# Attention weighting in a transformer block: split values as the stationary operand, two heads' probabilities moving, three branches summed in PSUM

## The reference, cut to what matters

```
# p_cmp: softmax over 31 compressed keys; p_sel, p_win: causal softmax over 512 keys
# (with 8 blocks of 64 keys and 16 to choose, every block is chosen, and a window of
#  512 covers all 512 keys: both are full causal attention, with keys and values of their own)
o_cmp = einsum('bghsn,bngd->bsghd', p_cmp, v_compressed)
o_sel = einsum(p_sel, v_sel);  o_win = einsum(p_win, v_win)
gate  = sigmoid(h @ w_gate)                      # 3 per head and token
y_nsa = gate[0]*o_cmp + gate[1]*o_sel + gate[2]*o_win
```

## Time and profile before

| | us |
|---|---|
| median of 3 runs | 2829.82 (2827.25 to 2831.1) |
| span of the profiled execution | 2832.2 |
| PE busy | 2781.4 (98%) |
| DVE busy | 2007.5 (71%) |
| ACT busy | 1158.5 (41%) |
| POOL busy | 62.7 (2%) |

### The profile page before, as it was taken

One profiled execution on the slowest core, in us unless ns is written; L12 is line 12 of the kernel. 1 busy time (PEld: TensorE's weight loads), 2 busy tenths in 40 slices (PEclk: granted clock), 3 DMA queues, 4 the chain that ended last, 5 costly groups with the idle time before them and its releaser, 6 DMA issues.

```text
span 2832.2 us, 41533 instructions
## 1 busy us (share of the span) xinstructions
PE 2781.4 (98%) x16782; PEld 2473.6 (87%) x16782; DVE 2007.5 (71%) x2956; ACT 1158.5 (41%) x1635; POOL 62.7 (2%) x22
## 2 busy tenths in 40 slices
PE   7999999999999999999999999999999999999998
PEld 7888888888888989789898899988999888789897
DVE  4456654544658969589694797875979588669794
ACT  4333444444243424334344443432434357434342
POOL 0000011111000000000000000000000000000000
PEclk9999999999999999999999999999999999999999
DMA  7223312222533333223333233332332343123322
GB/s 221 90 78 105 112 62 84 93 81 97 184 120 98 103 107 111 104 89 105 105 105 106 79 101 109 100 114 69 109 111 93 122 171 110 60 75 107 112 95 75
DMA packets 262192, 295.39 MB, mean 104 GB/s; under 512 B 6210, under 2 KB 248018, under 8 KB 259342
## 3 DMA queue, kind: packets, MB, share of 16 engines
q1 hardware_dynamic: 257008, 281.53, 30.3%
q10 hardware_dynamic: 5022, 11.57, 1.1%
HBM read 276.30 MB, written 16.78 MB: 103 GB/s over the span
## 4 chain that ended last, share of the span: by engine, by line
PE 75%; DVE 20%; issue 3%; ACT 1%; DMA 0%; DVEq 0%; ACTq 0%; SPq 0%
PE bank L1420 13%; PE bank L1422 12%; PE bank L1421 12%; PE bank L1863 5%; PE bank L1865 5%; PE bank L1864 5%; PE bank L1694 5%; PE bank L1752 2%; DVE gate_quarters_lo L2625 2%; DVE up_quarters_lo L2625 2%; PE bank L2026 1%; PE bank L1742 1%; DVE w_lo L2121 1%; PE bank L1435 1%; PE bank L1436 1%
## 5 line engine op out<-in xcount | busy, mean ns | idle before, releaser
L2121 DVE TENSOR_TENSOR w_lo<-w_raw,w_hi 128x2048 fp32r<-128x2048 f32 (+2 forms) x140 | 306.4, 2191 | 138.9 <-ACT w_hi L831 135.7
L1420 PE MATMUL bank<-hid_hi,w_hi 128*128 128x512 f32 x880 | 343.0, 390 | 0.0
L1421 PE MATMUL bank<-hid_lo,w_hi 128*128 128x512 f32 x880 | 342.5, 389 | 0.0
L1422 PE MATMUL bank<-hid_hi,w_lo 128*128 128x512 f32 x880 | 342.4, 389 | 0.0
L831 ACT ACTIVATE w_hi<-w_raw 128x2048 fp32r<-128x2048 f32 (+2 forms) x134 | 243.0, 1820 | 240.0 <-PE bank L1422 161.3
L1420 PE MATMUL bank<-h_hi,w_hi 128*128 128x512 f32 x752 | 298.6, 397 | 3.0 <-DVE w_lo L2121 1.4
L1421 PE MATMUL bank<-h_lo,w_hi 128*128 128x512 f32 x752 | 293.0, 390 | 0.0
L1422 PE MATMUL bank<-h_hi,w_lo 128*128 128x512 f32 x752 | 292.9, 390 | 0.0
L1422 PEld LDWEIGHTS bank<-hid_hi,w_lo 128*128 128x128 f32 x880 | 165.2, 188 | 34.5
L1421 PEld LDWEIGHTS bank<-hid_lo,w_hi 128*128 128x128 f32 x880 | 165.3, 188 | 33.7
L1420 PEld LDWEIGHTS bank<-hid_hi,w_hi 128*128 128x128 f32 x880 | 165.2, 188 | 33.8
(11 more groups left out here) (465 smaller groups left out, 6962.4 us busy)
## 6 DMA issues: line engine op xcount, KB each, us to landing
w_raw<-in_ffn_w_in_dram SPq DMA_DIRECT2D x88, 1024.0 KB, 5.0
w_raw<-in_ffn_w_out_dram SPq DMA_DIRECT2D x32, 1024.0 KB, 5.2
w_raw<-in_w_in_dram SPq DMA_DIRECT2D x28, 1024.0 KB, 5.1
w_raw<-in_w_ffn_in_dram SPq DMA_DIRECT2D x22, 1024.0 KB, 5.0
w_raw<-in_ffn_w_out_dram SPq DMA_DIRECT2D x16, 768.0 KB, 4.5
w_raw<-in_conv_w_pw_dram SPq DMA_DIRECT2D x12, 1024.0 KB, 6.6
phase_taps<-in_conv_dw_phases_dram SPq DMA_DIRECT2D x10, 1152.0 KB, 7.8
w_raw<-in_w_ffn_down_dram SPq DMA_DIRECT2D x8, 1024.0 KB, 5.2
```

What stands on the lines that cost most here:

```text
L1420: nc.tensor.matmul(bank[b][:, 0:n], wh, xh, start=first, stop=False)
L1421: nc.tensor.matmul(bank[b][:, 0:n], wh, xl, start=False, stop=False)
L1422: ins = nc.tensor.matmul(bank[b][:, 0:n], wl, xh, start=False, stop=last)
L2121: v.tensor_tensor(w_lo[slot][:, 0:n], raw[s][:, 0:n], w_hi[slot][:, 0:n].bitcast(F32), ALU.subtract).then_inc(w_lo_ready, 1)
```

## The change

The order of the steps becomes: query block (3 down to 0), pair of heads, branch, head. Sixteen turns j of two steps (one pair of heads, one branch) take the place of 32 steps; `it` counts the iterations of the loop, 18 in all. In iteration `it` PE makes the scores of turn it, transposes turn it-1 and weighs turn it-2.

- The values of the group are split on DVE into high and low and set side by side as a 128 x 128 stationary operand (`split_values`, `v_st`, `vc_st`), at the head of the group.
- DVE scales the probabilities by gate over row sum before they are turned (`scale_step`), instead of the sums after.
- The turned probabilities are split: ACT copies the high part (`high_step`), DVE makes the low part (`low_step`), for every step.
- `weigh` makes, for each key block, two fp32r matmuls with 256 moving columns (two heads), high and low; they accumulate over keys and both branches on top of the compressed branch (`cmp_turn`, `cmp_high`, `cmp_low`, `cmp_weigh`), which now goes with the loop, one query block and pair at a time. High and low values give two halves of the output's 128 partitions, which ACT and DVE add together (`out_copy`, `out_add`). The result is already turned (`y_sum`); it is split once after the loop.
- At a group's head DVE does all of the compressed softmax, the values' split and the first scaling before PE's first transpose; 18 gate products stand between (`GATE_FIRST`). Then six follow each iteration. ACT copies tiles 0 to 3 out in iterations 3, 7, 11 and 15.

The diff, cut to what is spoken of:

```diff
-STEPS = [(br, qb, hh) for br in range(2) for qb in reversed(range(TT)) for hh in range(HPG)]
+STEPS = [(br, qb, 2 * pair + h) for qb in reversed(range(TT)) for pair in range(2) for br in range(2) for h in range(2)]
+NJ = NS // 2
+SUMS = [(qb, pair) for qb in reversed(range(TT)) for pair in range(2)]
-GATE_CMP, GATE_STEP = 1, 3
-GATE_EVAC = {6: 0, 13: 1, 21: 2, 29: 3}
+GATE_CMP, GATE_FIRST, GATE_STEP = 1, 18, 6
+GATE_EVAC = {3: 0, 7: 1, 11: 2, 15: 3}
...
# ACT
-                for i in range(NS + 2):
-                    if i < NS:
-                        exp_step(i)
...
+                act.wait_ge(c_sh, g + 1)
+                nc.scalar.activation(p_c[:, :, :, :], p_c[:, :, :, :], ACT.Exp, scale=DH ** -0.5).then_inc(c_e, 1)
+                for it in range(NJ + 2):
+                    if 1 <= it <= NJ:
+                        high_step(2 * it - 2)
+                        high_step(2 * it - 1)
+                    if it < NJ:
+                        exp_step(2 * it)
+                        exp_step(2 * it + 1)
+                    if it % 2 == 1 and it < 2 * NA:
+                        cmp_high(it // 2)
+                    if it % 2 == 1 and it >= 3:
+                        out_copy((it - 3) // 2)
+                    if it in GATE_EVAC:
+                        gate_evac(GATE_EVAC[it])
+                        if GATE_EVAC[it] == 1:
                             high_in_loop(g * 2 + (U_NSA // 2 + 1), 0, 0, HALF)
+                        if GATE_EVAC[it] == 3:
                             high_in_loop(g * 2 + (U_NSA // 2 + 1), 1, 1, HALF)
...
# PE
+                def weigh(j):
+                    br, qb, _ = STEPS[2 * j]
+                    pe.wait_ge(s_pd, g * NS + (2 * j + 2))
                     for kb in range(qb + 1):
-                        ins = nc.tensor.matmul(bank[OUT_BANK[i // HPG % 2]][:, c:c + DH], probT[i % 4][:, kb * P:(kb + 1) * P],
-                                               v_sw[br][:, kb, bass.ds(g * DH, DH)], start=kb == 0, stop=kb == qb)
+                        for part in range(2):
+                            ins = nc.tensor.matmul(bank[OUT_BANK[j // 2 % 2]][:, 0:2 * P], v_st[br][:, kb, :],
+                                                   probT[j % 2][part][:, kb, :, :].rearrange("p h q -> p (h q)"),
+                                                   start=False, stop=j % 2 == 1 and kb == qb and part == 1)
...
+                for it in range(NJ + 2):
+                    if it < NJ:
+                        scores(2 * it)
+                        scores(2 * it + 1)
...
+                    if it == NJ - 1:
+                        pe.wait_ge(q_stored, 16 * GROUPS)
+                        gates(1).then_inc(c_t, 1)
+                    if 1 <= it <= NJ:
+                        turn(2 * it - 2)
+                        turn(2 * it - 1)
+                    if it % 2 == 1 and it < 2 * NA:
+                        cmp_turn(it // 2)
+                    if it >= 2:
+                        if it % 2 == 0:
+                            cmp_weigh(it // 2 - 1)
+                        weigh(it - 2)
+                    gates(GATE_FIRST if it == 0 else GATE_STEP)
                 gates(GATE_TILES * 3 * KT)
+                pe.wait_ge(s_or, g * NA + NA)
...
# DVE
+                cmp_max()
+                cmp_shift()
+                link(v.tensor_copy(gate_g.rearrange("p q h b -> p q (h b)"), gate[:, :, bass.ds(g * 3 * HPG, 3 * HPG)]))
+                mask_step(0)
+                mask_step(1)
+                cmp_sum()
+                cmp_gain()
+                cmp_mask()
+                split_values()
+                for it in range(1, NJ + 3):
+                    if it <= NJ:
+                        scale_step(it - 1)
+                    if it < NJ:
+                        mask_step(2 * it)
+                        mask_step(2 * it + 1)
+                    if it >= 4 and it % 2 == 0:
+                        out_add(it // 2 - 2)
+                    if it <= NJ:
+                        low_step(2 * it - 2)
+                        low_step(2 * it - 1)
+                    if it % 2 == 1 and it < 2 * NA:
+                        cmp_low(it // 2)
+                    if it == 9:
+                        compressed_keys(g + 1)
```

More of the change, by code:

```diff
@@ L1113, in merge @@
                 high_in_loop(c + (U_MERGE // 2 + 1), 0, 0)
+            act.wait_ge(s_or, NA * GROUPS)
+            act.wait_ge(q_stored, 16 * GROUPS)
+            for half in range(2):
+                tiles = slice(4 * half, 4 * half + 4)
+                nc.scalar.activation(ynsa[0][:, tiles, :], y_sum[:, tiles, :], ACT.Copy).then_inc(y_high, 1)
             merge(0)
@@ L1743, in turn, with cmp_turn @@
                     ins.then_inc(s_t, 1)
-                def weigh(i):
-                    br, qb, hh = STEPS[i]
-                    pe.wait_ge(s_pa if i % 2 == 0 else s_pd, g * (NS // 2) + (i // 2 + 1))
-                    if i % HPG == 0 and i >= 2 * HPG:
-                        pe.wait_ge(s_or, g * (NS // HPG) + (i // HPG - 1))
-                    c = DH * hh
+                def cmp_turn(a):
+                    qb, pair = SUMS[a]
+                    if a == 0:
+                        pe.wait_ge(c_p, g + 1)
+                    if a >= 2:
+                        pe.wait_ge(s_or, g * NA + (a - 1))
+                    for h in range(2):
+                        ins = nc.tensor.transpose(bank[OUT_BANK[a % 2]][0:NC, P * (2 + h):P * (3 + h)], p_c[:, qb, 2 * pair + h, :], ident)
+                    ins.then_inc(c_tu, 1)
@@ L1754, in weigh @@
                     ins.then_inc(s_o, 1)
-                for i in range(0, NS + 4, 2):
-                    if i < NS:
-                        scores(i)
-                        scores(i + 1)
-                    if i == 2:
-                        pe.wait_ge(m_lo_s, 4)
-                        pe.wait_ge(y_split, g * 2 + 2)
-                    if 2 <= i < NS + 2:
-                        turn(i - 2)
-                        turn(i - 1)
-                    if i >= 4:
-                        weigh(i - 4)
-                        weigh(i - 3)
-                    if i < NS + 2:
-                        gates(2 * GATE_STEP)
@@ L2343, in _ @@
                     steps[what](n)
-            dve.sem_inc(y_split, 2)
-            gate4 = gate[:, :, :].rearrange("p q (h b) -> p q h b", b=3)
+            for part in pT_c:
+                v.memset(part[:, :].bitcast(F32), 0.0)
+            v.memset(vc_st[:, :].bitcast(F32), 0.0)
             pc3 = p_c[:, :, :, :].rearrange("p q h n -> p (q h) n")
@@ L2442, in merge @@
                 if isinstance(c, int):
+                    for half in range(2):
+                        tiles = slice(4 * half, 4 * half + 4)
+                        dve.wait_ge(y_high, Y_HIGH + half + 1)
+                        v.tensor_tensor(ynsa[1][:, tiles, :], y_sum[:, tiles, :], ynsa[0][:, tiles, :].bitcast(F32), ALU.subtract
+                                        ).then_inc(y_split, 1)
                     dve.wait_ge(w_lo_ready, U_MERGE + 1)
```

220 lines of the change are left out of this document (103 added, 117 removed).

## The result

The changed kernel takes 2909.3 us (median of 4 runs, 2904.1 to 2913.3) against 2828.8 us (four runs) for the kernel before on the same chip: 1.028 times the time, 95% interval 1.027 to 1.030. It is slower, as forecast, but by 80 us and not by 30, and outside the range.

What follows compares the result with a forecast made beforehand. The prediction took the attention loop to be bound by PE's own instructions. It summed 59.0 us gone against 88.5 new (waits, clock), net +29.5 on the median 2829.8, giving 2860 us; range 2818 to 2895.

Steps and rivals of the forecast that it cites:

- PE's work: Attention loop: cheaper fp32r weightings and no transposes of the result take 10.9 us a group off PE, 43.6 in all.
- The gate tiles: Iterations 3, 7 and 11: PE waits for ACT's tile copies, 1.7, 1.6 and 1.6 us, 4.9 a group.
- Iteration 15: PE waits at tile 5's first product for POOL's low part of unit 3, idle 5.8 us a group.
- Head and ring: First transpose waits for DVE's scaling, 4.6 us a group, 1.3 more once; scaling-to-transpose chain in iterations 5, 9, 13, 1.5 a group.
- The next group's unit: Group's end: only the next group's queries were considered, behind iteration 15's load; counted as nothing, at most 2 us a group.
- The clock: PE's half clock behind waits longer than 2.00 us: 2.5 us each, two a group, 20 in all.
- slower still: Rival: the three short waits of each group pull the clock down too, 30 us more, 2890; chance 0.17.
- The rival in which the tiles don't wait: Rival: ACT reaches tile copies and unit 3 before PE wants them; 53 us less, 2807; chance 0.19.

Runs made afterwards that it cites:

- experiment 4: The changed kernel with the edits of experiment 1, experiment 2 and experiment 3 together: 2825.5 us, 0.999 of the kernel before.
- experiment 8: Experiment 4 plus values split at the group's start, iteration 1's gate products before the compressed transposes, compressed low part behind the next scaling: 2814.1 us, 0.9945 of before.
- experiment 3: The changed kernel with DVE's compressed sum, gain and masking behind the first scaling and the values' split behind the first low parts: 2908.1 us, 1.028 of before.
- experiment 5: The changed kernel with the edits of experiment 1 and experiment 2, its own order at the group's head kept: 2825.6 us, 0.998 of before.
- experiment 2: The changed kernel with ACT's high part of the next group's first unit made in iteration 15 instead of behind the loop: 2875.6 us, 1.017 of before.
- Experiment 6: The kernel before, attention untouched, with the next group's first weight unit split by ACT behind the copies of gate tiles 4 and 5: 2886.1 us, 1.020 of before.
- experiment 7: More gate products per narrow pair of compressed scores: two instead of one in the changed kernel, 2920.2 us; three in experiment 6's kernel, 2888.6 us.
- experiment 1: The changed kernel with ACT's copies of gate tiles 0 to 3 in iterations 1, 5, 9 and 13: 2854.1 us, 1.009 of before.
- experiment 9: Experiment 8 with three more gate products in iterations 1 and 5 each, taken from the group's end: 2824.9 us, 0.999 of before.

## Why the prediction was wrong

**PE's work: right, a little too much gain.** 39.2 us less at full clock by the table and 33 to 36 by experiments 4 and 8, 43.6 said. The new weightings stand where the prediction put them, 0.11 to 0.12 us apart:

```profile
443.00 0.28 PE L1805 MATMUL bank<-probT_high,v_win_stacked 128*128 128x256 f32 x1
443.11 0.28 PE L1805 MATMUL bank<-probT_low,v_win_stacked 128*128 128x256 f32 x1
```

**The gate tiles: right for the waits.** 12 waits, 24.0 us, 19.6 said (4.9 a group). What the clock lost behind them was not in the sum (below).

**Iteration 15: right.** Four waits of 6.1 us, 5.8 said, with the steps in the order of the prediction:

```profile
432.18 0.60 ACT L1106 ACTIVATE gate_stage<-bank 128x512 f32<-128x512 f32 x1
...
433.38 1.06 ACT L832 ACTIVATE w_hi<-w_raw 128x1024 fp32r<-128x1024 f32 x1 [0.60 <-ACT gate_stage L1106]
...
434.51 2.34 POOL L1418 TENSOR_TENSOR w_lo<-w_raw,w_hi 128x1024 fp32r<-128x1024 f32 x1 [29.47 <-ACT w_hi L832]
...
436.90 0.79 PE L1726 MATMUL bank<-h_hi,w_hi 128*128 128x512 f32 x1 [6.09 <-POOL w_lo L1418]
```

**Head and ring: too dear.** 14.5 us in all, 25.7 said (4 x 6.1 and 1.3). The head of group 0 waits 5.50 us, 5.9 said; those of groups 1 to 3 wait 1.2 to 1.7 for the first scaling. DVE's chain from the last compressed score to the first scaled probability took 8.8 us in group 1, 10.8 reckoned (POOL's low part did not meet it there); and PE's side of the comparison was reckoned at full clock, where in groups 1 to 3 it began at half of it (experiment 3). Experiments 4 and 5, nearly all at full clock, show the waits that the prediction meant: 32.3 and 29.8 us a loop. That the second is near the 25.7 is luck: its heads make 14.5 (19.7 said), since DVE's chain was priced too high, and the ring 15.3 (6.0 said).

**The next group's unit: not in the sum, and this step failed.** The prediction looked for who stands behind the wait in iteration 15, and found the queries ("at most 2 us a group"). It did not ask what stands behind the new last instruction of ACT's loop, the copy of the last sum, which ends with PE's last weighting. Cost: 15.8 us of waits at three group starts and the merge, and their clock; experiment 2 gets back 33.7 us by moving this one call.

**The clock: 20 us said, 50.3 measured. This is the larger failure.** The prediction took 2.5 us for each long wait, a mean over groups of the kernel before, and gave that to two waits a group, the head's and iteration 15's. Added up from the stretches at 0.50 in the trace of the changed kernel, half of PE's busy time in each (51.0 us in all; the 50.3 comes from stretches of 2 us):

| clock's loss, us | predicted | measured |
|---|---|---|
| behind iteration 15 | 10 | 9.9 |
| behind the heads' waits | 10 | 1.4 |
| behind the tile waits | 0 | 17.0 |
| behind the group's starts | 0 | 22.7 |

So two things were wrong. The price of a wait depends on what runs behind it: behind iteration 15, where mostly wide products follow, 0.50 lasted from 436.9 to 443, 3 us lost (the last three rows below); behind the group's start it lasts 14 to 16 us, 7 to 8 lost, since the compressed scores are mostly matmuls of 32 columns. Experiment 6 measures that price by itself (7.4 us), and experiment 7 shows that it goes with the share of narrow matmuls. And waits of about 2 us, which the prediction left without a price, were mostly followed by falls: behind 10 of the 12 tile waits the clock went to 0.50 for some 3 us, 1.7 us lost each. In group 0 it did so behind the tile waits of iterations 7 (1.95 us, first row below) and 11, and not behind that of iteration 3 (2.10 us). Its rival "slower still" had just that mechanism, at 30 us where it cost 17, and its 2890 was the nearest number on the page, still 19 us short, because the group's start was missing in it too.

```profile
403.00:404.00 1.00, 1.00 (x7) 0.50 0.00 0
...
434.00:436.00 2.00, 0.00 (x0) 0.50 0.25 92
436.00:443.00 7.00, 6.10 (x17) 0.50 0.71 238
443.00:445.00 2.00, 2.00 (x11) 1.00 1.01 343
```

The Trainium skill (TensorE: Matmul & The Clock Gate, Part 1) says that the clock is held down by default and that sustained activity releases it. The traces agree on the first half: with every wait of over 3 us in the loops of these kernels the clock was at 0.50 in the wait or within 1.2 us behind it. On the second they say more: in experiment 6 two stretches, one behind the other, with PE busy 8.00 of 8.00 us stood at 0.50 and 0.52, so that PE is busy without a break in the profile did not by itself bring the clock back.

**The rivals.** The rival in which the tiles don't wait is experiment 1, near enough: it gained 55 us, 53 said, for that step. The agreement is luck: the sum was 43 for the waits and 10 for the clock, and the trace has 48 for the waits and 25 for the clock, of which DVE's ring took 13 back. And its base was too low by the unit and the clock, so even so the kernel stays slower than before.

## What to carry to other kernels

When a loop body gets shorter on the bounding engine, the tables and the order that place the other engines' side jobs (copies, weight preparation) are out of date at once: list every job whose result PE needs, with the instruction that now stands ahead of it, the last one of each loop included. Price a wait by what follows it: a wait of 6.1 us ahead of wide matmuls cost 9 in all, one of 4.2 ahead of narrow ones 12. And expect the next engine to take up what is won: here waits for DVE took all of the 8 us a group until its own order was mended too, and close to 5 after that.

## What the runs showed of the hardware

- *Half clock through a narrow stretch.* Behind a wait of 3.2 to 7.8 us, pairs of 32-column matmuls with one 512-column product between them ran at 0.50 for 14 to 18 us, in all nine group starts of the changed kernel, of experiment 1 and of experiment 6. With three products between them it was 3.8 to 6.4 us, and with mostly or only wide products behind the wait (iteration 15, the merge) 2.9 to 6.2. A short wait can be enough: in experiment 9 one of 0.9 us was followed by 17 us at 0.50, two of 1.0 us by none. Entered at full clock, the same stretch stays at 1.00 (group 2 of experiment 8, 76.84 us at 1.00).
- *POOL holds DVE's scaling and splitting by `tensor_scalar` as well.* The prediction had this from one row of a two-input instruction. In experiment 8 the split of the values, on one input, took 2.04 us beside POOL's low part where it takes 0.29 alone, and a scaling pair 1.45 where it takes 0.60. POOL and DVE in order of time, the pair at 578.94 with no POOL instruction beside it:

```profile
574.55 2.36 POOL L1419 TENSOR_TENSOR w_lo<-w_raw,w_hi 128x1024 fp32r<-128x1024 f32 x1 [24.86 <-ACT w_hi L832]
...
575.80 1.45 DVE L2452 TENSOR_SCALAR prob<-prob,nsa_stat 128x128 f32<-128x128 f32 x2
...
578.94 0.60 DVE L2452 TENSOR_SCALAR prob<-prob,nsa_stat 128x128 f32<-128x128 f32 x2
...
581.56 4.60 POOL L1419 TENSOR_TENSOR w_lo<-w_raw,w_hi 128x2048 fp32r<-128x2048 f32 x1 [4.66 <-ACT w_hi L832]
...
584.27 2.04 DVE L2399 TENSOR_SCALAR v_sel_stacked<-v_sel 128x256 fp32r x1
```

The first ends 0.3 us behind POOL's instruction, the second 0.15 behind. A reciprocal at 575.60, beside POOL too, took its usual 0.17. The Trainium skill (SBUF — State Buffer, section Who interferes with whom) names `tensor_scalar` in its two-port form among those that can be held; these rows agree, though none shows in which form it ran. In group 0 of experiment 8 the same contention makes the subtraction of the compressed softmax 4.87 us long:

```profile
359.75 4.54 POOL L1419 TENSOR_TENSOR w_lo<-w_raw,w_hi 128x2048 fp32r<-128x2048 f32 x1 [359.30 <-ACT w_hi L832]
...
359.96 4.87 DVE L2417 TENSOR_TENSOR p_cmp<-p_cmp,nsa_stat 128x496 f32<-128x496 f32 x1
```

- *Open.* Why the clock came back after 4.5 us in one group and after 21.5 and 22.5 in two others of the same kernel, with two products to a pair, was not settled.
